# Latent attention scores as three products of rounded parts, pairwise squares at the entry, and a reordered first border in a one-core hybrid layer kernel

## The reference

```
h = rms_norm(x) * (1 + sc) + sh;  x = x + 0.5 * g * rms_norm(swiglu(h, w_in, w_out))   # 1st and 3rd
mixer: one input projection; mLSTM branch hm; attention branch ha
  q, k = rms_norm per head (16 q heads, 4 kv heads, 64 wide), latent tokens get axial rotary positions
  latent queries read 512 latent keys and 128 cached keys in one softmax; prompt queries read prompt keys
  y = sigmoid(g0) * (hm @ w_bm) + sigmoid(g1) * (ha @ w_ba);  out = y @ w_out
```

## Time and profile before

| | us |
|---|---|
| median of three runs | 1703.99 |
| profiled execution | 1704.33 |
| its span in the trace | 1702.6 |
| PE busy in the span | 1679.4 |
| DVE busy | 1044.2 |
| ACT busy | 745.3 |

### The profile page before, as it was taken

How to read it: one execution, slowest core, us unless ns; L and a number is a source line. 1 busy time by engine, 2 the same in 40 slices (tenths; PEclk the granted TensorE clock), 3 DMA queues, 4 the chain that set the end, 5 groups by cost and what they waited for, 6 DMA issues and landing times.

```text
span 1702.6 us, 27823 instructions
## 1 busy us (share of the span) xinstructions
PE 1679.4 (99%) x11327; PEld 1545.3 (91%) x11327; DVE 1044.2 (61%) x1779; ACT 745.3 (44%) x1402; POOL 0.2 (0%) x4
## 2 busy tenths in 40 slices
PE   8999999999999999999999999999999999999998
PEld 6998899989889888999999888889889989998997
DVE  5777687548666224555537877775646834872775
ACT  6312255325574332443445554553564433551452
POOL 0000000000000000000000000000000000000000
PEclk9999999999999999999999999999999999999999
DMA  9787222322613215233243211111621221332233
GB/s 386 279 319 262 75 66 84 100 61 89 210 54 111 84 62 113 82 95 87 81 149 118 67 52 42 42 41 58 228 87 50 75 87 62 100 97 77 74 105 144
DMA packets 56790, 189.66 MB, mean 111 GB/s; under 512 B 7464, under 2 KB 16472, under 8 KB 53848
## 3 DMA queue, kind: packets, MB, share of 16 engines
q1 hardware_dynamic: 56664, 187.89, 33.1%
HBM read 170.67 MB, written 16.54 MB: 110 GB/s over the span
## 4 chain that ended last, share of the span: by engine, by line
PE 89%; DVE 4%; ACT 3%; issue 1%; DMA 0%; DVEq 0%; ACTq 0%
PE psum L762 9%; PE psum L764 9%; PE psum L763 9%; PE psum L744 7%; PE psum L745 7%; PE psum L746 7%; PE psum L872 4%; PE psum L873 4%; PE psum L874 4%; PE psum L1288 2%; PE psum L1270 2%; PE psum L834 2%; PE psum L836 2%; PE psum L835 2%; PE psum L1248 2%; PE psum L1173 1%
## 5 line engine op out<-in xcount | busy, mean ns | idle before, releaser
L1906 DVE TENSOR_TENSOR wlo<-raw,whi 128x1024 fp32r<-128x1024 f32 x120 | 146.8, 1224 | 310.4 <-ACT whi L1382 310.3
L1382 ACT CAST whi<-raw 128x1024 fp32r<-128x1024 f32 x120 | 125.5, 1046 | 257.2 <-PE psum L874 125.1
L762 PE MATMUL psum<-g_hi,whi 128*128 128x320 f32 x656 | 209.4, 319 | 0.2 <-ACT gate L1724 0.2
L764 PE MATMUL psum<-g_hi,wlo 128*128 128x320 f32 x656 | 202.7, 309 | 0.0
L763 PE MATMUL psum<-g_lo,whi 128*128 128x320 f32 x656 | 202.6, 309 | 0.0
L762 PEld LDWEIGHTS psum<-g_hi,whi 128*128 128x128 f32 x656 | 123.2, 188 | 4.9 <-issue 1.9
L872 PE MATMUL psum<-whi,g_hi 128*128 128x512 f32 x320 | 125.0, 390 | 0.0
L874 PE MATMUL psum<-whi,g_lo 128*128 128x512 f32 x320 | 124.5, 389 | 0.0
L873 PE MATMUL psum<-wlo,g_hi 128*128 128x512 f32 x320 | 124.5, 389 | 0.0
L763 PEld LDWEIGHTS psum<-g_lo,whi 128*128 128x128 f32 x656 | 123.3, 188 | 0.7
L764 PEld LDWEIGHTS psum<-g_hi,wlo 128*128 128x128 f32 x656 | 123.1, 188 | 0.0
(11 more groups left out here) (446 smaller groups left out, 4386.2 us busy)
## 6 DMA issues: line engine op xcount, KB each, us to landing
raw<-in_w_ffn_in SPq DMA_DIRECT2D x88, 512.0 KB, 3.6
raw<-in_w_mix SPq DMA_DIRECT2D x77, 512.0 KB, 4.1
raw<-in_w_ffn_out SPq DMA_DIRECT2D x44, 512.0 KB, 3.6
direct<-in_w_mod SPq DMA_DIRECT2D x7, 2048.0 KB, 9.4
mw<-in_w_mod SPq DMA_DIRECT2D x14, 768.0 KB, 5.4
mw<-in_w_mod SPq DMA_DIRECT2D x8, 1024.0 KB, 16.8
gate<-gate_keep SPq DMA_DIRECT2D x24, 320.0 KB, 5.2
gate_keep<-gate SPq DMA_DIRECT2D x20, 320.0 KB, 4.6
```

The source lines that it names most:

```text
L762: mm(out, wh[:, k, :], hi[:, k, cols], start=(k == 0), stop=False)
L764: last = mm(out, wl[:, k, :], hi[:, k, cols], start=False, stop=(k == nk - 1))
L1382: copy((to or whi[t.slot])[:, :, :], raw[t.raw][:, :, :]).then_inc(w_hi, 1)
L1906: tt(lo[:, :, :], raw[t.raw][:, :, :], hi[:, :, :].bitcast(F32), ALU.subtract).then_inc(raw_free, 1)
```

## The change

- Entry: ACT writes all eight squares to buffers of their own (`x_sq`); DVE adds them in pairs ((0,1), (2,3), (0,2), (4,5), (6,7)); PE takes three partial sums in turn. `split(Tile(0))` comes after the root. Ten idle products instead of 12, and none between the sums.
- `SUM_AFTER`: sum 2 after tile 8 instead of 9, sum 3 after tile 12 instead of 11. After tiles 8 and 12 there is a direct group already.
- First border: SP loads post-norm rows and then all of x_tok after all border tiles and before the mixer's tiles. Border tiles 3 and 4 are split within the last group of seven, ahead of `pair_high` on ACT and `pair_low` on DVE (this holds for the last border too). The mixer's first two tiles are split in row 0, the next in rows 1 and 2. Row 0 takes its last four steps by tile.
- Scores: the cached keys are loaded into the first 128 columns of `ak`, whose prompt keys go to `akp` before. ACT and DVE split keys (4 x 128x640) and latent queries (8 x 128x512) into high and low parts; a latent block takes 12 fp32r products of 320 columns. `fill(0)` is done ahead of `scores(0)`. The high keys lie where gates 4 to 7 were, so the ring of gates has four buffers after the first eight.

```diff
+    if l == 0 and c == 0:
+        return [s for p in pairs for s in p] + [(f, nj - 2 + o) for f in range(2) for o in range(2)]
...
+        k_hi = at("k_hi", [P, 2 * NKC, N], F32R, x_at + 4 * row)
+        k_lo = at("k_lo", [P, 2 * NKC, N], F32R, mw_at)
+        q_hi, q_lo = m_hi, m_lo
...
-                    if c == T_MIX - 3:
-                        sp.wait_ge(prod_done, KEEP + 5 * (FIRST_PAIRS[2] - 1) + 4)
-                        load_tokens(slice(0, 2))
-                load_tokens(slice(2, NT))
+                load_post(0)
+                sp.dma_start(x_tok[:, :, :].rearrange("p c d -> p (c d)"), a["x_tok"]).then_inc(x_back, 16)
...
             def first_stats():
-                pe.wait_ge(sq_sum, KC - 1)
-                for h in range(2):
-                    last = mm(half_out(2, h), ones_d, rb[:, HCOLS[h]], start=True, stop=True)
+                for count, k in ((3, 0), (4, 4), (5, 6)):
+                    pe.wait_ge(sq_sum, count)
+                    for h in range(2):
+                        last = mm(half_out(2, h), ones_d, x_sq[:, k, HCOLS[h]], start=(k == 0), stop=(k == 6))
...
                 if k < KC:
-                    pe.wait_ge(rope_out, NKC + m + 1)
+                    pe.wait_ge(qk_lo, KC + 2 * NKC + m + 1)
...
-                    for b in range(2):
-                        for s in range(2):
-                            mm(psum[:, 2 * s, 2 * b * P:2 * (b + 1) * P], aq[half[s], m, c * P:(c + 1) * P],
-                               ak[half[s], key[s], TP + 2 * b * P:TP + 2 * (b + 1) * P], start=True, stop=True)
-                    for s in range(2):
-                        last = mm(psum[:, 2 * s + 1, 0:PAST], aq[half[s], m, c * P:(c + 1) * P],
-                                  akc[half[s], g, :], start=True, stop=True)
+                    for h in range(2):
+                        for n, (q, kk) in enumerate(((q_hi, k_hi), (q_hi, k_lo), (q_lo, k_hi))):
+                            for s in range(2):
+                                out = flat(s)[:, KEY_AT + h * HALF:KEY_AT + (h + 1) * HALF]
+                                last = mm(out, q[half[s], m, tok], kk[half[s], key[s], HCOLS[h]], start=(n == 0), stop=(n == 2))
...
+            def key_high(n):
+                if n == 0:
+                    act.wait_ge(ak_sw, 80)
+                    act.wait_ge(ck_in, 32)
+                    act.wait_ge(gate_used, KC)
+                copy(k_hi[:, n, :], ak[:, n, :]).then_inc(qk_hi, 1)
...
+            for n in range(2 * NKC):
+                key_low(n)
...
+            query_low(0)
+            query_low(1)
             top(0, 0)
             top(0, 1)
             turn_halves(QK - 1)
...
+                if k + 2 < KC:
+                    query_low(k + 2)
                 divide(k)
```

More of the change, by code:

```diff
@@ L1241, in scores @@
                             last = mm(psum[:, 2 * s, j * P:(j + 1) * P], aq[half[s], 4 * m + j, 0:TP],
-                                      ak[half[s], key, 0:TP], start=True, stop=True)
+                                      akp[half[s], key, :], start=True, stop=True)
                 else:
@@ L1347, in _ @@
                 pe.wait_ge(ev[t.slot], t.pair + 1)
+            fill(0)
             scores(0)
             qk_stats(QK - 1)
-            fill(0)
             fill(1)
@@ L1444, in seven @@
                         split(Tile(base + 2 * n + 4), row_weights(2 * net(base), 2, base + 2 * n + 2)[0], 0)
+                        for u in range(3, 5):
+                            split(t.plus(u), row_weights(2 * net(base), u, t.c)[0], ut.n + 3)
                     else:
@@ L1514, in border @@
                 ended = Tile(base - 1).n + 3
-                for u in range((3, 5, 3)[l], ROW_TILES[l]):
+                for u in range(5, ROW_TILES[l]):
                     if l == 1 and u == 6:
@@ L1530, in border @@
                     root_y(l, c, base)
[L1531 to L1535, removed]
+                    if c == 0 and l < 2:
+                        first_split(0, ended)
+                        first_split(1, ended)
+                    elif l == 0 and c < 3:
+                        first_split(c + 1, ended)
                     if l == 2:
@@ L1558, in first_normed @@
                 take_rows(0)
+                split(Tile(0))
                 for k in range(KC):
@@ L1584, in _ @@
                 act.wait_ge(ld_x[X_PART[k]], 16)
-                reuse(0, k)
-                fn(sq[k % 2][:, :], x[:, k, :], ACT.Square).then_inc(ysq_in, 1)
-            split(Tile(0))
+                fn(x_sq[:, k, :], x[:, k, :], ACT.Square).then_inc(ysq_in, 1)
             act.wait_ge(ystat_mm, 1)
@@ L1782, in _ @@
                 done(t)
+                if l == L_BM - 1:
+                    query_high(0)
                 if l < L_AK:
@@ L1831, in exponentials @@
                 if c:
-                    last = fn(sa[s][:, :], flat(s)[:, 0:N], ACT.Exp, bias=amax[:, s:s + 1], accum_out=asum[:, s:s + 1])
+                    last = fn(sa[s][:, :], flat(s)[:, KEY_AT:KEY_AT + N], ACT.Exp, bias=amax[:, s:s + 1], accum_out=asum[:, s:s + 1])
                 else:
@@ L1840, in gate_of @@
             def gate_of(i):
-                act.wait_ge(gate_in[i % KC], 16 * (i // KC + 1))
-                fn(gate[i % KC][:, :], gate[i % KC][:, :], ACT.Tanh, scale=0.5).then_inc(gate_sg, 1)
+                gate_ready(act, i)
+                fn(gate_of_slot(i)[:, :], gate_of_slot(i)[:, :], ACT.Tanh, scale=0.5).then_inc(gate_sg, 1)
+            query_high(1)
             inv_rms(QK - 1)
@@ L1848, in _ @@
             for k in range(PAIRS):
+                if k + 2 < KC:
+                    query_high(k + 2)
                 take_p(k)
@@ L1989, in seven @@
                     pair_product(n, s)
-                    if not rows_next:
+                    if rows_next:
+                        for u in range(3, 5):
+                            split(Tile(base + 2 * n + 2 + u), row_weights(2 * net(base), u, base + 2 * n + 2))
+                    else:
                         split(Tile(base + 2 * n + 3))
@@ L2088, in first_normed, with add_squares @@
                         mod_step(k - FIRST_K)
[L2090 to L2094, removed]
-                    dve.wait_ge(sq_sum, (KC - 1) * l + m - 1)
-                    tt(rb[:, :], rb[:, :], sq[m % 2][:, :], ALU.add).then_inc(sq_sum, 1)
+            def add_squares(one, two):
+                if two % 2:
+                    dve.wait_ge(ysq_in, two + 1)
+                else:
+                    dve.wait_ge(sq_sum, two)
+                tt(x_sq[:, one, :], x_sq[:, one, :], x_sq[:, two, :], ALU.add).then_inc(sq_sum, 1)
             def border(l, base, nxt):
@@ L2156, in first_split @@
                     split(Tile(nxt + u), first_weights(l, u, nxt))
-                for u in range((3, 5, 3)[l], ROW_TILES[l]):
+                for u in range(5, ROW_TILES[l]):
                     split(Tile(base + u), row_weights(l, u, base))
-                if l == 0:
-                    first_split(0)
-                    first_split(1)
                 for c in range(NT if l < 2 else NT - 1):
@@ L2258, in _ @@
                               ALU.add).then_inc(cols_in, 1)
-            for m in range(KC):
-                add_square(0, m)
-            split(Tile(0))
+            for one, two in ((0, 1), (2, 3), (0, 2), (4, 5), (6, 7)):
+                add_squares(one, two)
             root_ready(0)
@@ L2637, in _, with key_low, query_low @@
                     low_m(KC - 1)
+            def key_low(n):
+                dve.wait_ge(qk_hi, KC + n + 1)
+                tt(k_lo[:, n, :], ak[:, n, :], k_hi[:, n, :].bitcast(F32), ALU.subtract).then_inc(qk_lo, 1)
+            def query_low(m):
+                dve.wait_ge(qk_hi, KC + 2 * NKC + m + 1)
+                tt(q_lo[:, m, TP:N], aq[:, m, TP:N], q_hi[:, m, TP:N].bitcast(F32), ALU.subtract).then_inc(qk_lo, 1)
+            for n in range(2 * NKC):
+                key_low(n)
             def top(k, s):
@@ L2851, in lay_out @@
         "m0": f("state_m")[0, 0].T, "state_C": f("state_C"), "state_n": f("state_n"),
-        "cache_k": np.tile(f("cache_k").reshape(PAST, KVH, HD).transpose(2, 1, 0).reshape(HD, KVH * PAST), (2, 1)),
+        "cache_k": np.concatenate([f("cache_k").reshape(PAST, KVH, HD)[:, order].transpose(2, 1, 0).reshape(HD, KVH * PAST)
+                                   for order in ([0, 2, 1, 3], [1, 3, 0, 2])]),
         "cache_v": f("cache_v").reshape(PAST, KVH * HD),
```

83 lines of the change are left out of this document (47 added, 36 removed).

## The result

The changed kernel takes 1709.34 us in the median of nine runs (1707.11 to 1711.56), the kernel before 1704.34 beside it. The ratio is 1.0031, 95% interval 1.0022 to 1.0040: slower, by some 5 us. The profiled execution took 1709.52, with a span of 1707.8, 5.2 more than before.

The account below looks back on a forecast made before the run. PE was taken as the bound, busy 1679.4 of 1702.6 us. Gains in steady scores and costs at the attention's start and first pairs, with small other terms, summed to +1.0 on 1704.33: 1705.3 us, range 1697 to 1714.

Parts of the forecast that it names:

- the third case: Dearer attention start: start +5.35, clock low twice +2.9, first pairs +1.8, border 0; 1708.6 us, chance 0.18.
- 31 steady blocks: Attention's latent blocks after the first: paired fp32r products make each block's scores 0.19 us shorter, -5.9 in all.
- start to `turn_p(0)`, clock included: Attention start: scores(0) wait for key and query copies, +5.35 us; half clock behind PE's wait, +1.2.
- first pairs: Attention pairs 0 to 5: query copies fill DVE, which sets the time in two or three, +1.0 us.
- first border: First border: earlier normed(0) against two splits added to the row ring, and less slow clock, -0.5 us.
- sums: Sums moved beside direct groups: 0.3 us saved for each of two, 0.5 wait for DVE, -0.1.
- entry: Entry: statistics about 1.8 us earlier, but the load of part 4 sets the time, -0.05.
- One reading of the sum: Old steady block's scores: paired float32 passes at 0.213 and 0.107 us, 1.07 in all, at 1/2.4 ns per column.
- ACT's branch: Attention start: ACT's exponentials after the inverse root end near 971.3 us and are not last before `turn_p(0)`.
- 3.9 of 5.2 us: First attention pairs: DVE's steady busy time against a pair's length, before query and weight splits are added.
- the signs: Trace marks that would show the forecast right or wrong, among them sum 2 waiting 0.4 us for DVE.

Follow-up runs that it names:

- experiment 4: Changed kernel with nine idle products on PE ahead of scores(0): 1708.67 us in one run.
- experiment 6: Changed kernel with each query's high and low parts formed one pair earlier: 1706.13 us, ratio 1.0009 to the kernel before.
- experiment 1: Kernel before with only the scores' part of the change: 1709.87 us, ratio 1.0035.
- experiment 2: Kernel before with only the entry, sums and first border of the change: 1704.85 us, ratio 1.0001.
- experiment 9: Changed kernel with all four mixer splits moved into waits behind the norm and row sum, and x_tok loaded in two parts: 1702.61 us, ratio 0.9992.
- experiment 3: Changed kernel with the score products ordered in threes by half of the array instead of in turn: 1709.14 us in one run.
- experiment 7: Changed kernel with the splits of mixer tiles 2 and 3 moved behind the norm on ACT and the row sum on DVE: 1708.78 us in one run.
- 5: Changed kernel with high and low keys formed one per projection tile, earlier, only the fourth key_low left at the end: 1706.62 us, ratio 1.0015.
- 8: Changed kernel with mixer splits 2 and 3 moved into waits and seven idle products ahead of the first turn_rows: 1705.76 us in one run.
- 11: Changed kernel with early keys, queries one pair earlier, splits in waits, x_tok in two loads, four idle products, query_low(2) behind invert(0): 1697.05 us, ratio 0.9953.

## Why the prediction was right in range and wrong in its middle

The prediction said 1705.3 with 1697 to 1714, and "same" as likeliest; it was 1709.34 and slower by more than 0.2%. "Slower" had 0.32 in all. The time lies nearest to the third case, to which it gave 0.18, with 1708.6, but the steps aren't quite its steps: it had the clock at 2.9 (1.7 measured) and the first pairs at 1.8 (4.3 measured), and these two errors partly cancel. Step by step, against the profiled execution:

| step | predicted | measured |
|---|---|---|
| 31 steady blocks | -5.9 | -6.6 (31 x 0.212), with 0.6 of it not in the steady part |
| start to `turn_p(0)`, clock included | +5.35 + 1.2 | +6.90 |
| first pairs | +1.0 | +4.3 |
| first border | -0.5 | +0.84 |
| sums | -0.1 | -0.27 |
| entry | -0.05 | -0.66 |
| sum | +1.0 | +5.2 |

**Steady blocks: right.** Two products on the two halves cost 0.145 together, as the full-array product did. The Trainium skill ("TensorE: Matmul & The Clock Gate", section "Part 3: Packing small matmuls — row/col tiling") says that a weight load overlaps running products only where its group of array rows differs. By that, loads would be laid bare here. The trace doesn't agree: both halves are loaded anew for every two products, and these start every 0.145 us. Of the 0.6, 0.2 is the gain of scores(1), which lies ahead of `turn_p(0)` and so within the +6.90. The other 0.4 is missing around the two prompt pairs: from `turn_p(23)` to `turn_p(27)` it is 23.42 instead of 23.62, where three latent scores should have given 0.64. Why was not tried. One reading of the sum was wrong without harm: two float32 products of 256 columns do start every 0.213 or so, but at one column per 1/2.4 ns that would be 0.107; each takes two such times per column.

**The start: right, but for one reading.** scores(0) at 965.6 foretold and 965.59 measured, the wait in front of it 4 us, the clock at half behind it. Without the low clock `turn_p(0)` stands at 972.43 (experiment 4), where the sum without the clock had 972.8; with it at 974.27. The clock's 1.74 was put at 1.2, which is what 3.4 us of it cost; here it was low for 6.8. One reading failed by it: ACT's branch was to end near 971.3 and not last, but with the statistics at half clock it ended at 973.1 and DVE's inversion waited 0.53 for it.

**The first pairs: the step that failed.** The prediction weighed DVE's load against the length of a pair, "3.9 of 5.2 us", and put the excess at 1.0, 1.8 at most. (A pair took 5.64 us before, with 4.2 of DVE; no row shows 5.2.) What counts is when within the pair the low query is ready: scores(k + 2) follow values(k) at once, and query_low(k + 2) stands behind the split and the fill. Its 0.6 us alone would be little, but it makes the whole of DVE's pair a thing that PE waits for: 0.53, 1.61, 0.98 and 0.53 us at scores(2) to scores(5). With the same work one pair earlier the loss is 0.9 (experiment 6). The code that shows this order was there to be read.

**The border: right in kind, its size not settled.** normed(0) was to be 2.2 earlier by its estimated 467.9; it began at 468.60, since the mixer's second tile landed at 467.6 and its split stands ahead on ACT, and the first turned row was 1.04 earlier against the start of the border. The prediction counted 0.5 MB of post-norm rows ahead of that tile; the trace has two loads of 512 KB, and 0.5 MB more at the 383 GB/s of the earlier trace rows would be 1.4 us, an estimate. The splits in rows 1 and 2 cost 0.94 each instead of 1.05. So -1.04 + 1.88 = +0.84. But by experiment 1 the border of before varies by 0.9 as well, so whether the change as a whole costs or gives anything there isn't shown. The 1.77 us wait became one of 0.78. The low clock behind the old wait went, but PE's wait at `turn_rows` grew to 3.15, where a low clock is again possible: experiment 2 had one there, the changed kernel's profile had none.

**Sums and entry: small, as said.** Sum 2 waited 0.41 for DVE (0.5 in the sum, 0.4 among the signs). Part 4 landed 0.6 earlier, at 28.30, after an issue 0.26 earlier, and was used as it landed; the prediction had taken its issue as unmoved. In the twelve kernels with the new entry it is used at 27.74 to 28.92, in the two with the old one at 29.00 (before) and 29.09 (experiment 1), so this is the entry's doing, though its size varies.

## What to carry to other kernels

An operand made just in time is priced by its place: find who waits for it and what stands ahead of it on its engine, before comparing loads. A gain on an engine that then waits in one piece for several microseconds may be spent twice, as wait and as a low clock behind it; fill the wait or move work out of the chain that ends it. Splits and copies belong where the engine waits for another anyway: two splits in a ring of rows cost 1.9 us, and in its waits nothing that the rows show (9.1 us apart in experiment 9). And a step of less than 1 us that loads can move isn't settled by one profile on each side.

## What was not expected of the hardware

- Products of 64 rows on the two halves of the array start in pairs even when three of one half stand ahead of three of the other in the program (experiment 3).
- Much the same wait of PE ahead of `turn_rows` (3 to 4 us) was followed by half clock for 0 us (changed kernel), 3.4 us (experiment 2) and 6.8 us (experiment 7) in one profile each, and with the very same border code for 0 us in experiment 6 and 3.4 us in experiments 3, 4 and 5 (in 5 it began 1.5 us later). A single profile doesn't tell what such a wait costs; behind idle products there was none at the same place in all three kernels that had them (4, 8 and 11), though in experiment 4 one came some 7 us later and took back 0.98 us.
- Half clock also came without a wait ahead of it, in the mixer near 590 us, in work that no kernel here changes. From `first_half` to the last `qk_stats` of the projections it is 456.1 to 456.5 us where there was none (four profiles), 457.4 to 458.1 with 3.4 us of it (eight, before and the changed kernel among them) and 459.6 to 459.7 with 6.8 us (experiments 5 and 6). So such a stretch costs some 1.6 us of time, and spans of single profiles differ by as much for that alone.
